# Keeping the split Strassen weight sums of a down projection in DRAM after the first token group

## The reference, cut to what matters

```python
def ffn_sublayer(x, g_pre, w_up_l, w_down_l, g_post):
    h = rmsnorm(x, g_pre)
    a = jax.nn.relu(jnp.einsum('btd,df->btf', h, w_up_l))
    return x + rmsnorm(jnp.einsum('btf,fd->btd', a * a, w_down_l), g_post)
```

## Time and profile before

| | |
|---|---|
| median of 3 runs | 2645.64 us (2641.29 to 2654.81) |
| the profiled execution's own time | 2644.41 us |
| its span | 2642.6 us |
| mean granted TensorE clock | 0.984 |
| busy over the span: matmul / VectorE / ScalarE / GpSimd | 95% / 52% / 44% / 54% |
| DRAM read / written | 390.50 MB / 120.53 MB |
| group 0 of the feed-forward part | from about 1043 us to 1386 us |
| group 1 / group 2 / group 3 | 1386 to 1795 / 1795 to 2220.5 / 2220.5 to the end |

### The profile page before, as it was taken

The page is one execution under the profiler, slowest core; times in us unless marked ns, Lnnn a source line. Parts: engine busy times, 40 slices in busy tenths (PEclk is TensorE's granted clock), DMA queues, the critical chain, the costliest instruction groups (busy, mean ns, idle before and its releaser), DMA issues.

```text
span 2642.6 us, 35400 instructions
## 1 busy us (share of the span) xinstructions
PE 2522.6 (95%) x13562; PEld 2167.4 (82%) x13562; DVE 1382.9 (52%) x2231; ACT 1166.3 (44%) x2002; POOL 1415.2 (54%) x818
## 2 busy tenths in 40 slices
PE   7999999999999999999998999998999999999995
PEld 6899999899996468778877788777778778889884
DVE  6431221265663225865566554676555476655657
ACT  4000110187775534545454444554544455444443
POOL 1216560068663566665566675666665475554555
PEclk9999999999999999999999999999999999999998
DMA  5316764299988944564556555456555263553452
GB/s 183 112 44 244 264 230 120 83 164 180 166 146 212 295 160 166 193 208 159 167 183 242 176 168 183 151 170 232 173 173 193 99 235 120 198 178 127 142 191 96
DMA packets 297903, 457.65 MB, mean 173 GB/s; under 512 B 81748, under 2 KB 202140, under 8 KB 290776
## 3 DMA queue, kind: packets, MB, share of 16 engines
q1 hardware_dynamic: 270546, 313.71, 41.3%
q10 hardware_dynamic: 14518, 89.43, 9.5%
q0 software_dynamic: 12672, 52.24, 5.9%
HBM read 390.50 MB, written 120.53 MB: 193 GB/s over the span
## 4 chain that ended last, share of the span: by engine, by line
PE 76%; DVE 10%; DMA 5%; POOL 3%; ACT 3%; issue 2%; SPq 0%; ACTq 0%; DVEq 0%; POOLq 0%
PE ml_y L2171 13%; PE ml_up L2095 8%; PE ml_up L2096 8%; PE ml_up L2097 8%; PE ml_y L2128 6%; PE pj_acc L518 6%; PE pj_acc L519 6%; PE pj_acc L520 6%; PE at_o L1187 5%; PE at_turn L1167 2%; POOL ml_w_lo L1983 2%; DVE ml_a_lo L2479 2%; DVE ml_a_lo_raw L2451 2%; DVE ml_w_lo L2485 2%; PE at_score L1156 2%
## 5 line engine op out<-in xcount | busy, mean ns | idle before, releaser
L1983 POOL TENSOR_TENSOR ml_w_lo<-em_raw,ml_w_hi 128x1024 fp32r<-128x1024 f32 x296 | 741.2, 2512 | 635.1 <-ACT ml_w_hi L2203 634.9
L2203 ACT CAST ml_w_hi<-em_raw 128x1024 fp32r<-128x1024 f32 x384 | 401.4, 1046 | 295.8 <-PE ml_y L2171 189.0
L2095 PE MATMUL ml_up<-ml_h_hi,ml_w_hi 128*128 128x512 f32 (+2 forms) x1280 | 457.1, 357 | 23.3 <-POOL ml_w_lo L1983 23.3
L2096 PE MATMUL ml_up<-ml_h_lo,ml_w_hi 128*128 128x512 f32 (+2 forms) x1280 | 453.5, 354 | 0.0
L2097 PE MATMUL ml_up<-ml_h_hi,ml_w_lo 128*128 128x512 f32 (+2 forms) x1280 | 452.6, 354 | 0.0
L2171 PE MATMUL ml_y<-ml_w_hi,ml_a_hi 128*128 128x512 f32 x896 | 358.2, 400 | 34.4 <-DVE em_hx L2513 13.8
L2171 PE MATMUL ml_y<-ml_w_lo,ml_a_hi 128*128 128x512 f32 x896 | 352.6, 393 | 0.0
L2171 PE MATMUL ml_y<-ml_w_hi,ml_a_lo 128*128 128x512 f32 x896 | 352.3, 393 | 0.0
L2095 PEld LDWEIGHTS ml_up<-ml_h_hi,ml_w_hi 128*128 128x128 f32 x1280 | 243.2, 190 | 66.3 <-POOL ml_w_lo L1983 35.3
L518 PE MATMUL pj_acc<-pj_h_hi,pj_w_hi 128*128 128x424 f32 (+1 forms) x800 | 290.3, 363 | 5.6 <-DVE pj_h_lo L736 5.6
L519 PE MATMUL pj_acc<-pj_h_lo,pj_w_hi 128*128 128x424 f32 (+1 forms) x800 | 283.5, 354 | 0.0
(11 more groups left out here) (319 smaller groups left out, 4559.8 us busy)
## 6 DMA issues: line engine op xcount, KB each, us to landing
em_raw<-in_w_up SPq DMA_DIRECT2D x64, 1024.0 KB, 6.2
em_raw<-scratch_wt SPq DMA_DIRECT2D x128, 512.0 KB, 4.7
em_raw<-in_w_down SPq DMA_DIRECT2D x96, 512.0 KB, 3.7
out_o_a_k_s<-in_cache_a_k ACTq DMA_DIRECT2D x8, 3060.0 KB, 11.9
out_o_a_v_s<-in_cache_a_v ACTq DMA_DIRECT2D x8, 3060.0 KB, 13.2
em_raw<-scratch_pt SPq DMA_DIRECT2D x34, 512.0 KB, 7.3
pj_work<-in_w_down POOLq DMA_DIRECT2D x16, 1024.0 KB, 6.3
scratch_wt<-pj_work POOLq DMA_DIRECT2D x16, 1024.0 KB, 4.5
```

The costliest lines, as they stand in the source:

```text
L1983: nc.gpsimd.tensor_tensor(split_of(w_lo, n), raw_of(n), f32(split_of(w_hi, n)), ALU.subtract).then_inc(w_lo_ready, 1)
L2095: pe.matmul(out, hi[:, k, :], h_hi[:, k, cols], start=(k == 0), stop=False)
L2096: pe.matmul(out, hi[:, k, :], h_lo[:, k, cols], start=False, stop=False)
L2203: nc.scalar.copy(split_of(w_hi, n), raw_of(n)).then_inc(w_hi_ready, 1)
```

## The change

The split halves of the weight sums (P7, P6, P5, P4) are kept. In group 0 they are split as before; then SyncE's queue stores both halves, hi and lo, to a new DRAM scratch tensor `ws`: 8 parts x 4 products x 2 stores of 512 KB. In groups 1 to 3 these units have no raw load, no ScalarE copy and no low split: at the place of the unit's `split_hi`, ScalarE issues two DMAs of 512 KB, hi and lo, straight into the two slots. VectorE does no low split in groups 1 to 3 any more (the new test `g == 0` in `lo_by_dve`), so that of P3 goes to GpSimd there. A slot that held a saved unit is not overwritten until its stores have landed. In groups 1 to 3 a raw load holds P1 and P2, another P3.

```diff
--- before.py
+++ after.py
@@ -1604,8 +1604,10 @@
         kind, g, part, i = step
         if kind != "down" and i % 2 == 0:
             LOADS.append((step, (kind, g, part, i + 1)))
-        if kind == "down" and i in (P1, P2, P5):
+        if kind == "down" and g == 0 and i in (P1, P2, P5):
             LOADS.append((step, (kind, g, part, i + 1)))
+        if kind == "down" and g and i == P1:
+            LOADS.append((step, (kind, g, part, P2)))
         if kind == "down" and i == P3:
             LOADS.append((step,))
     for n, load in enumerate(LOADS):
@@ -1710,6 +1712,8 @@
         w_hi_ready = ph.sem("w_hi_ready")
         w_lo_ready = ph.sem("w_lo_ready")
         w_lo_by_dve = ph.sem("w_lo_by_dve")
+        w_saved = ph.sems("w_saved", SPLIT)
+        w_fetched = ph.sems("w_fetched", SPLIT)
         filled = ph.sem("filled")
         turn_hi = ph.sem("turn_hi")
         emptied = ph.sem("emptied")
@@ -1813,15 +1817,41 @@
 
         def lo_by_dve(n):
             kind, g, part, i = UNITS[n]
-            return kind == "down" and i in (LO_BY_DVE_LAST if part == LAST else LO_BY_DVE)
+            return kind == "down" and g == 0 and i in (LO_BY_DVE_LAST if part == LAST else LO_BY_DVE)
 
         DVE_LOS = [sum(lo_by_dve(m) for m in range(n + 1)) for n in range(NU)]
 
+        def fetched(n):
+
+            kind, g, part, i = UNITS[n]
+            return kind == "down" and g > 0 and i in SUM
+
+        def saved(n):
+
+            kind, g, part, i = UNITS[n]
+            return kind == "down" and g == 0 and i in SUM
+
+        HIS = [sum(not fetched(m) for m in range(n + 1)) for n in range(NU)]
+        FETCHES = [sum(fetched(m) for m in range(n % SPLIT, n + 1, SPLIT)) for n in range(NU)]
+        SAVES = [sum(saved(m) for m in range(n % SPLIT, n + 1, SPLIT)) for n in range(NU)]
+
+        def wait_hi(engine, n):
+            engine.wait_ge(w_hi_ready, HIS[n])
+
         def wait_lo(engine, n):
-            if lo_by_dve(n):
+            if fetched(n):
+                engine.wait_ge(w_fetched[n % SPLIT], 32 * FETCHES[n])
+            elif lo_by_dve(n):
                 engine.wait_ge(w_lo_by_dve, DVE_LOS[n])
             else:
-                engine.wait_ge(w_lo_ready, n + 1 - DVE_LOS[n])
+                engine.wait_ge(w_lo_ready, HIS[n] - DVE_LOS[n])
+
+        def wait_slot(engine, n):
+
+            if n >= SPLIT:
+                wait_used(engine, n - SPLIT)
+                if saved(n - SPLIT):
+                    engine.wait_ge(w_saved[n % SPLIT], 32 * SAVES[n - SPLIT])
 
         def wait_loaded(engine, load):
             engine.wait_ge(raw_in[load % RAW], LANDED[load])
@@ -1934,13 +1964,25 @@
             load_part(sp, d, early, MERGED_EARLY)
             load_part(sp, d, early, MERGED_EARLY + 1)
             load_convs(sp, 1)
-            for load in range(RAW, len(LOADS)):
-                load_raw(load)
-                if load == 4:
-                    sp.dma_start(gain_post[:], d["g_mix_post"].partition_broadcast(P)).then_inc(gain_in, 16)
-                    sp.dma_start(gain_pre[:], d["g_mlp_pre"].partition_broadcast(P)).then_inc(gain_in, 16)
-                if load == 8:
-                    sp.dma_start(gain[:], d["g_mlp_post"].partition_broadcast(P)).then_inc(const_in, 16)
+            def save(n):
+                kind, g, part, i = UNITS[n]
+                wait_hi(sp, n)
+                sp.dma_start(d["ws"][part, SUM[i], 0], f32(w_hi[:, n % SPLIT, :])).then_inc(w_saved[n % SPLIT], 16)
+                wait_lo(sp, n)
+                sp.dma_start(d["ws"][part, SUM[i], 1], f32(w_lo[:, n % SPLIT, :])).then_inc(w_saved[n % SPLIT], 16)
+
+            load = RAW
+            for n in range(NU):
+                while load < len(LOADS) and UNIT_OF[LOADS[load - RAW][-1]] <= n:
+                    load_raw(load)
+                    if load == 4:
+                        sp.dma_start(gain_post[:], d["g_mix_post"].partition_broadcast(P)).then_inc(gain_in, 16)
+                        sp.dma_start(gain_pre[:], d["g_mlp_pre"].partition_broadcast(P)).then_inc(gain_in, 16)
+                    if load == 8:
+                        sp.dma_start(gain[:], d["g_mlp_post"].partition_broadcast(P)).then_inc(const_in, 16)
+                    load += 1
+                if saved(n):
+                    save(n)
             for j in CLOSING_ORDER[0:2]:
                 load_res(sp, "x1", NG - 1, j)
             sp.wait_ge(early.merged, 2 * TILES)
@@ -1977,9 +2019,9 @@
                 nc.gpsimd.tensor_tensor(at, at, res[0:m, u % 2, :], ALU.add).then_inc(res_used, 1)
 
             def split_lo(n):
-                if n >= NU or lo_by_dve(n):
+                if n >= NU or lo_by_dve(n) or fetched(n):
                     return
-                pool.wait_ge(w_hi_ready, n + 1)
+                wait_hi(pool, n)
                 nc.gpsimd.tensor_tensor(split_of(w_lo, n), raw_of(n), f32(split_of(w_hi, n)),
                                         ALU.subtract).then_inc(w_lo_ready, 1)
 
@@ -2192,14 +2234,25 @@
         @block.scalar
         def _(act):
 
+            def fetch(n):
+                kind, g, part, i = UNITS[n]
+                wait_slot(act, n)
+                if (g, part, i) == (1, 0, P7):
+                    for slot in range(SPLIT):
+                        act.wait_ge(w_saved[slot], 32 * SAVES[NU - 1 - (NU - 1 - slot) % SPLIT])
+                act.dma_start(f32(w_hi[:, n % SPLIT, :]), d["ws"][part, SUM[i], 0]).then_inc(w_fetched[n % SPLIT], 16)
+                act.dma_start(f32(w_lo[:, n % SPLIT, :]), d["ws"][part, SUM[i], 1]).then_inc(w_fetched[n % SPLIT], 16)
+
             def split_hi(n):
                 if n >= NU:
+                    return
+                if fetched(n):
+                    fetch(n)
                     return
                 step = UNITS[n]
                 kind, g, part, i = step
                 wait_loaded(act, LOAD_OF[step])
-                if n >= SPLIT:
-                    wait_used(act, n - SPLIT)
+                wait_slot(act, n)
                 nc.scalar.copy(split_of(w_hi, n), raw_of(n)).then_inc(w_hi_ready, 1)
 
             def hi_mix(step):
@@ -2481,7 +2534,7 @@
             def split_lo(n):
                 if n >= NU or not lo_by_dve(n):
                     return
-                dve.wait_ge(w_hi_ready, n + 1)
+                wait_hi(dve, n)
                 nc.vector.tensor_tensor(split_of(w_lo, n), raw_of(n), f32(split_of(w_hi, n)), ALU.subtract).then_inc(w_lo_by_dve, 1)
 
             def lowered(frm):
@@ -3167,6 +3220,7 @@
 
 
 SCRATCH = {
+    "ws": (FF // P // 4, 4, 2, P, D),
     "pt": (FBLK, P, TOK),
     "kv": (TOK, D),
     "oct": (2, P, TOK),
```

## The result

The changed kernel takes 2701.05 us in the median (2697.86 to 2704.89, 4 runs), the kernel before 2646.07 on the same chip: ratio 1.0205, 95% interval 1.0174 to 1.0236. It is 55 us slower, where 2644.0 was forecast with a range up to 2664.

The account below looks back on a forecast made before the run. TensorE was taken as the bound, with only its 50.7 us of waits in groups 1 to 3 and clock falls to win. 26.8 us won less 25.2 lost took 1.6 from 2645.6: 2644.0 us, range 2624 to 2664.

Parts of the forecast that it names:

- Group 0: Group 0's 64 stores of 512 KB on SyncE's queue: each lands in 2.8 us; cost nothing, up to 8 us.
- Rival D: Group 0 pays for its stores with 8 us and more, on top of the forecast: 2652 and up, chance 0.08.
- The fetch behind a cache copy: P6's fetch waits behind the copy on ScalarE's queue: 6.0 us (parts 4, 6), 2.6 (part 2), 0.4 (part 0); group 3 none.
- P5 and P4: Their fetches in groups 1 to 3 have at least as much time to land as P6's 8.1 us.
- P7: Its fetch in groups 1 to 3 lands in 5.1 to 6.2 us, under the 6.73 available: costs 0 to little.
- Rival B: Fetches late in every part beside raw loads, up to 9.2 us; P7 late costs 20 to 40 us: 2664 or more, chance 0.17.
- The gain: Groups 1 to 3, from VectorE's low splits removed and the clock's return: 26.8 us, bounds 15 and 33.
- the 20.0 of the sum: TensorE's waits for VectorE in groups 1 to 3 that go: 20.0 of 28.9 us.
- the 5.3 that the fetch replaced: Two P6 waits for VectorE in part 2, left out of the gain because the fetch takes their place.
- The clock's 6.8 us: Part of the gain: clock coming back in the two 60 us stretches at 0.94, 6.8 taken of 7.2 us.
- GpSimd's order: Groups 1 to 3: residual adds behind P3's split delay up 2 in six places, 11.2 us, between 5 and 16.
- The clock: Loss from two clock falls among some 11 new waits: 3.5 us, 0 to 12.

Follow-up runs that it names:

- Experiments 1: The changed kernel with group 0's stores only, groups 1 to 3 loading and splitting as in the kernel before: 2681.82 us, ratio 1.0124.
- 3: The changed kernel with each saved unit's stores issued ahead of the raw loads on SyncE's queue: 2670.47 us, ratio 1.0099.
- 8: The changed kernel with the cache copies of all four groups at unit P5, stores still behind the raw loads: 2670.32 us, ratio 1.0098.
- experiment 10: The changed kernel with both halves of P6 fetched from SyncE's queue instead of ScalarE's in groups 1 to 3: 2693.66 us, ratio 1.0166.
- experiments 4: The changed kernel with the cache copies of groups 1 to 3 moved from up 3 to unit P5: 2655.90 us, ratio 1.0045.
- 5: The control: the kernel before, with only the cache copies of groups 1 to 3 moved from up 3 to P5: 2635.33 us, ratio 0.9962.
- experiment 7: The changed kernel with stores ahead of raw loads, and in groups 1 to 3 copies at P5 and P3's low split on VectorE: 2616.53 us, ratio 0.9896.
- 6: The changed kernel with stores ahead of raw loads and the cache copies of groups 1 to 3 at P5: 2626.48 us, ratio 0.9925.

## Why the prediction was wrong

**The step that failed** is "Group 0", with "Nothing, up to 8 us" for the stores. It cost 34.2 us. The landing was taken from the one store in the earlier trace rows, 2.8 us, and the check against the DMA share of a regular part. The regular part did keep its 41.3 us, but the landing was wrong even there: in part 3 of group 0 the low stores of P7, P6, P5 and P4 took 7.7, 2.6, 7.0 and 8.7 us, and the median of all 32 is 7.9. What was left out was that P7's store goes out 1.8 us ahead of the cache copy, and behind two raw loads. The copy was priced for fetches of groups 1 to 3 on its own queue, but the same copy is issued in group 0 also, and it holds stores on the other queue, to 15.8 to 16.4 us. Experiments 1 (34 us with the stores alone), 3 (28 of them back by order alone) and 8 (a different unit pays when the copy is elsewhere) show this. Rival D named group 0 with "8 us and more", at 0.08. The sum of group 0: 20.4 us of waits at P6, and 13.7 us that TensorE was busy for longer (349.2 us, 335.4 before) at a clock of 0.96 in place of 1.00.

**"The fetch behind a cache copy"** was right in place and too small in size. Predicted: part 0 0.4 beyond a wait already there, part 2 1.3, parts 4 and 6 1.5 each. The waits in group 1 are 7.9 (7 was expected for the unit itself), 4.9, 3.3 and 3.7 us. The term that was mis-sized is the time behind the copy: the fetch was given 2.2 us after the copy's landing, and in groups 1 and 2 it landed 3.3 to 4.4 us after it in parts 4 and 6, 5.9 in part 2 and 6.8 in part 0. The copies themselves got longer in group 0 alone, 13.5 to 15.4 us from 11.5 to 12.2; in group 1 they took 11.7 to 13.8 us, 11.5 to 15.2 before. The reason given, the queue, was a minor part (experiment 10). Moving the copies (experiments 4 and 5) shows some 32 us between them, clock included, against 9.0 in the sum. In group 3 P6 had room, as said, but for part 0 (2.2 us).

**P5 and P4** were given "at least as much" cover as P6. The cover was right, 8.2 us; the landing was not. P4's fetch goes out beside a raw pair of 1 MB, 2.7 us behind P5's, and takes 7.5 to 9.0 us in groups 1 and 2, and 10.9 to 11.1 where an `x1` store and a residual load lie between. That cost 3.3 and 3.2 us in the two part 5s and up to 1.2 elsewhere. The prediction took P4's landing as if its fetch ran alone.

**P7** was right: 4.5 to 5.9 us to land, no wait. Rival B, which had P7 late in half of the parts or more, did not come. Its mechanism did, at another unit: with a raw load of 1 MB alongside it gave a fetch up to 9.2 us, and P4's, the one that has such a load beside it, took 7.5 to 9.0 in groups 1 and 2.

**The gain** was right. TensorE's waits for VectorE fell from 28.9 to 4.4 us, so the 20.0 of the sum came, and most of the 5.3 that the fetch replaced. The clock's 6.8 us did not, since the fetch waits made new falls. With those mostly gone (experiment 7) groups 1 and 2 take 394 and 406 us, 11 and 5 less than in the control, which is what is left of the gain after 14.8 us of fetch waits. GpSimd's splits, which the prediction said would get shorter, took 2.50 us in the mean of groups 1 to 3 both before and after. **GpSimd's order**, 11.2 us of waits with the clock's share beside it, was sized too high: experiment 7 against 6 shows 9.9 us in all, of which 4.6 are waits of up units. In the change itself such waits are 1.7 us at most, likely because the late P4 or P6 ahead of them left GpSimd time; no run shows that cause by itself. **The clock** was given 3.5 us. Its share shows in TensorE's busy time, which grew by 4 us in groups 1 and 2 together and by the 13.7 us above in group 0. TensorE stood idle 2 to 8 us each time before it fell in groups 0 to 2. Summed, the waits of groups 1 to 3 went from 52.0 to 69.0 us, where the forecast had them about even; these 17 us and the clock's are the 20 us by which the three groups grew.

## What to carry to other kernels

Before adding transfers, write down what other large DMA is issued within some 15 us on any queue, and price the new ones at that place and not by their median; a store that frees a buffer is on the path as much as a load. Issue the store that frees a slot ahead of the bulk loads that nobody waits for yet, since order on a queue costs no work and was worth 28 us here. When a change seems to fail, run the same rearrangement on the old kernel too: here a quarter of what moving the copies gained had nothing to do with the change's own idea.

## What was not expected of the hardware

A DRAM-to-DRAM copy of 3060 KB, 12 to 14 us in the median, delays small transfers of both queues that carry weights: fetches of 1 MB in groups 1 and 2 from 4.6 us to between 10.9 and 17.3, stores of 512 KB to 16.4. In the packet records it goes out in 48 packets of 65,280 bytes, 2.9 us each in the median, and a fetch in packets of 4096 bytes. No run here cuts the copy into smaller packets. With no copy near, P7's low store landed in 3.1 us when it stood ahead of the raw loads (part 1, experiment 3) and in 7.9 us behind them (part 1, the change). A fetch of 1 MB lands in 4.6 us alone, in 5.5 when another was issued 2.3 us before, and in 7.5 to 10.2 when a raw pair of 1 MB was issued up to 1.8 us before as well (the change). Seven of the 24 issues of P6's low half on SyncE's queue, those beside a copy in parts 4 and 6 of groups 1 and 2 and parts 2, 4 and 6 of group 3, took 4.1 to 6.7 us, where the others took 0.3 to 0.7 (experiment 10).
